# A hybrid decoder layer on one core: order of the first two weight tiles, and when the copies for the down sums are issued

## The chip, the cores and the metric

The kernel runs on one core of a Trainium2 chip. Its engines are TensorE (PE in the profile; PEld is its weight load), VectorE (DVE), ScalarE (ACT), GpSimd (POOL) and SyncE (SP), and 16 DMA engines that all queues share. The metric is the time of one execution in microseconds (us); lower is better. A kernel's time is the median of its runs.

## The reference

One decoder layer in float32 on 1024 tokens of width 1024, with 16 learned meta tokens put ahead of them:

```
h = concat([meta, x])                         # 1040 rows
proj = rmsnorm(h, norm1) @ w_in               # D_IN columns, cut into twelve parts
gdn = gated_delta(silu(conv4(gq, gk, gv)), ga, gb);  ret = retention(rotary(rq), rotary(rk), rv)
y = sigmoid(gate_a) * norm(gdn) * silu(gz) + sigmoid(gate_b) * silu(rg) * norm(ret)
h = h + y @ w_out
u = conv3(rmsnorm(h, norm2) @ w_up) + b;  a, b = split(u)
h = h + (silu(a) * b) @ w_down                # w_down is (2816, 1024)
out = rmsnorm(h, norm_f)[16:]
```

## The kernel before

**Layout.** Columns of h lie along the free axis and its channels in 8 blocks k of 128 partitions, so that a projection tile t is 128 output columns: its weights are 8 blocks of 128x128, and it needs every block of x. For accuracy each float32 operand is split into a high and a low part, and each product is three matmuls: high by high, low by high, high by low. `w_hi` is made on ScalarE (L1511), `w_lo` on VectorE (L1894), both from `w_raw`, which SP loads (512 KB, L822). Two slots hold the split weights, tile t in slot t % 2; `w_raw` has one.

**The start** (step "intro"). SP loads the 8 blocks of x. ScalarE makes `xh` of each (L1527) and its square (L1533), VectorE makes `xl` (L1916, semaphore `x_split`) and adds up the squares (L1911, `d_xss`). TensorE works on tiles 0 and 1 together while the blocks arrive; a block of a tile is 9 matmuls (`project_block`, L155), three thirds of the columns by three products. The function `first_two(s, ks)` does the blocks ks of tile s. At one place in this order stand the "ones matmuls" (L1180), which sum the squares over the channels. From their result ScalarE takes a logarithm (L1545) and an exponential (L1548); VectorE folds these roots into the rotary tables (L1942) and then does the rotary work of tiles 0 and 1 (L1946 to L1956). After it in VectorE's order stands the low split of tile 3.

**The steady state** (steps "proj", "split", "load" of a plan that all engines follow in one order). A tile is three units of 24 matmuls (L1148), one for each third of the columns. Behind each unit ScalarE copies its bank out (L1586). In the first unit of tile t ScalarE and VectorE split tile t+1, and SP issues the load of tile t+2, which waits until tile t+1 is split. Every second tile has rotary work on VectorE and two stores of 522 KB; from tile 10 on turned keys are stored too, 16 small stores for each pair of tiles (L789, L791), which SP issues ahead of the load.

**The down sums.** Late in the kernel the down projection uses sums of quarters of `w_ffn_down` (a11, a12, a21, a22, each 1408 rows of 512 columns). GpSimd prepares four of them in device memory (`down_sums`): four copies of a quarter each (L2526, 2816 KB each, device memory to device memory), issued when TensorE has finished tile 4, and from tile 65 on additions into them. `w_sums` counts all of these transfers, 16 for each; the later waits on it begin with the copies' count.

Of the kernel before, what the change touches and what calls it, by code (L numbers as in the profile page):

```python
# [17 lines left out]
KC = D // P  # L18
# [29 lines left out]
KH = FT // 2  # L48
# [59 lines left out]

BATCH = 4
NBATCH = 3  # L110
B32 = 32
INV_STEPS = 2 + 2 * (B32 - 1)

# [7 lines left out]
def shape_constants():  # L121
# [6 lines left out]
    c[:, C_EPSQ] = EPS * EPS * P  # L128
    c[:, C_BLK:C_BLK + 4] = i[:, None] // B32 == np.arange(4)[None, :]
    upto = i[:, None] <= i[None, :]  # L130
    c[:, C_TRIU:C_TRIU + P] = upto
    c[:, C_UPTO:C_UPTO + P] = np.where(upto, 0, -1e30)
    c[:, C_BELOW:C_BELOW + P] = np.where(i[None, :] < i[:, None], 0, 1e30)
    c[:, C_L5:C_L5 + 64] = -1.0 * (i[:, None] % 64 // B32 == i[None, 0:64] // B32)
    lg = np.log(1.0 - 2.0 ** (-5.0 - np.arange(RH)))
# [43 lines left out]
def front_plan():  # L179
# [52 lines left out]
    u = 34  # L232
    for b in range(NBATCH):
        steps[u].append(("tin", b))
        if b == 1:
            steps[u + 4].append(("comp", NCH - 1))
        j = 0
        while j < B32 - 1:
            u += 1
            n = min(B32 - 1 - j, 2 if u < 49 or u % 2 else 3)  # L240
            steps[u].append(("inv", b, j, j + n))
# [138 lines left out]
def third_columns(t, j):  # L380

    if t >= T_ZB or t < 8:
        return C_COL + C_N * j, C_N
    if T_Q <= t < T_V:

        return T - 344 * (3 - j), 344
    if T_K <= t:
        return (FRONT, FRONT + 348, FRONT + 694)[j], (348, 346, 346)[j]
    return N3 * j, N3
# [11 lines left out]
def program(nc, io, sc, out):  # L401

    with ExitStack() as ctx:
# [10 lines left out]
        def sem(name):  # L414
            return ctx.enter_context(nc.semaphore("f1_" + name))
# [112 lines left out]
        def w_parts(t):  # L528
# [4 lines left out]
            if 6 <= n < 8:  # L533
# [15 lines left out]
        comp, mb, xb, xc, xt = (ext[:, 5632 + 1024 * n:6656 + 1024 * n] for n in range(5))  # L549
        mbv, xbv = (x.rearrange("p (a b) -> p a b", a=B32) for x in (mb, xb))  # L550

# [11 lines left out]
               for n in range(2)]  # L563
# [7 lines left out]
        w_hi, w_lo, units_done, evac, pe_x15, d_fold = (sem(n) for n in (  # L571
            "w_hi", "w_lo", "units_done", "evac", "pe_x15", "d_fold"))
# [15 lines left out]
        d_dec, a_dec, a_eg, w_sums, pe_qk, d_attn, pe_lev, d_q5, d_x5, d_t6, a_q6, d_x6 = (  # L588
            sem(n) for n in ("d_dec", "a_dec", "a_eg", "w_sums", "pe_qk", "d_attn", "pe_lev", "d_q5", "d_x5", "d_t6",
                             "a_q6", "d_x6"))  # L590
# [40 lines left out]
        def sums_stored(j):  # L631

            return 16 * (NCH + (j + 1 if j < KH else KH + 3 * (j + 1 - KH)))
# [71 lines left out]
        def col(tab):  # L705
            return tab.rearrange("p (h o) -> p h o", o=1)
# [37 lines left out]
        def used(q):  # L744

            return (d_bank, q // KH + 1) if q % KH == KH - 1 else (d_used, (KH - 1) * (q // KH) + q % KH + 1)
# [21 lines left out]
        def tiles_done(t):  # L768
            return 3 * t + 3
# [5 lines left out]
        def _(sp):  # L775
# [22 lines left out]
            for step in plan:  # L798
                kind, a = step[0], step[1:]
# [30 lines left out]
                elif kind == "rvstore":  # L830
                    u = a[0]
                    at0, n, chunks = RV_STEPS[u - RV_A]
# [15 lines left out]
                elif kind == "kturn":  # L848
                    n = a[0] - T_K
                    store_turned(sc["kt"], n, kt, kt0, d_kt, 2 * n + 2, kt_st)  # L850
                elif kind == "vturn":
                    n = a[0] - T_V
# [70 lines left out]
                elif kind == "dl_x":  # L923
                    c = a[0]
                    if c == 0:
                        sp.wait_ge(x_st, 32 * NBATCH)
                    if c >= 2:
                        sp.wait_ge(p_exp, 2 * c - 3)
                    cols = slice(256 * (c % BATCH), 256 * (c % BATCH) + 256)
                    for odd in range(2):  # L930
                        for n in range(2):
                            to, of = 64 * odd + B32 * n, 64 * n
# [25 lines left out]
                elif kind == "dl_k":  # L958
# [3 lines left out]
                    elif c == 0:  # L962
                        sp.wait_ge(kt_st, 16 * 8 * KC)
                        sp.wait_ge(d_tout, 2 * NBATCH)
                    sp.dma_start(kd[c % 2].rearrange("p h c -> p (h c)"), sc["kt"][c]).then_inc(kd_ld, 16)
# [12 lines left out]
                elif kind == "oload":  # L978
                    n = a[0]
# [14 lines left out]
                elif kind == "gate" and a[0] < 8:  # L994
                    n = a[0]
# [49 lines left out]
            def down_operands(q):  # L1045
                p, k = q // KH, q % KH
                w = io["w_ffn_down"][0]
                first, second = w[k * P:k * P + P, :], w[(KH + k) * P:(KH + k) * P + P, :]
                into_w = (first[:, 0:512], sc["ws"][1, k], second[:, 0:512], sc["ws"][0, k], sc["ws"][2, k], sc["ws"][3, k],
                          second[:, 512:1024])[p]  # L1050
                into_a = (sc["act"][k][:, 0:512], sc["ts"][1, k], sc["act"][KH + k][:, 0:512], sc["ts"][0, k],
                          sc["ts"][2, k], sc["act"][KH + k][:, 512:1024], sc["ts"][3, k])[p]
                return into_w, into_a

            def load_down(q):
                p, k = q // KH, q % KH
                if q == KH:
                    sp.wait_ge(w_sums, 16 * (4 + 3 * KH))
                elif q == 5 * KH:
                    sp.wait_ge(w_sums, 16 * (4 + 4 * KH))  # L1060
                if q >= DIN:
                    sp.wait_ge(da_hi, q - DIN + 1)
                j = k if p == 0 else KH + k
                sp.wait_ge(act_st[j % 2], 16 * (j // 2 + 1))
                if p:
                    sp.wait_ge(sum_st, sums_stored(j))
                if q < DW:
                    sp.wait_ge(pe_p, 7 * (NPAIR - 1) if q < DEARLY else 7 * NPAIR)
                else:
                    sp.wait_ge(*used(q - DW))  # L1070
                for into, of in zip((dw_raw[q % DW], da_raw[q % DA]), down_operands(q)):
                    sp.dma_start(into[:, :], of).then_inc(dn_in[q % DIN], 16)
# [11 lines left out]
            for i in range(NPAIR):  # L1084
                j = J0 + i
# [26 lines left out]
        def _(pe):  # L1112
# [6 lines left out]
            for step in plan:  # L1119
                kind, a = step[0], step[1:]  # L1120
                if kind == "proj":
                    t, j = a
                    u = 3 * t + j
                    if T_RV <= t < T_Q:
                        pe.wait_ge(w_lo, T_RV + (4 if u < RV_B else 6 if u < RV_C else 8))
                        pe.wait_ge(evac, u - 1)
                        at0, n, chunks = RV_STEPS[u - RV_A]
# [17 lines left out]
                    at0, n = third_columns(t, j)  # L1145
# [15 lines left out]
                elif kind == "intro":  # L1161
                    pe.wait_ge(w_lo, 1)

                    def first_two(s, ks):
                        for k in ks:
                            pe.wait_ge(x_split, k + 1)
                            mm = project_block(pe, psum, 2 + 3 * s, wh[s], wl[s], xh, xl, k, 0, N3)
                            if k == KC - 1:
                                mm.then_inc(units_done, 3)

                    for k in range(KC // 2):
                        first_two(0, (k,))
                        if k == 0:
                            pe.wait_ge(w_lo, 2)
                        first_two(1, (k,))
                    first_two(0, range(KC // 2, KC))
                    pe.wait_ge(consts_in, 16)
                    pe.wait_ge(d_xss, KC - 1)
                    for bank, at0, c0, c1 in XSS:
                        mm = pe.matmul(psum[:, bank, at0:at0 + c1 - c0], ones, post[4][:, c0:c1], start=True, stop=True)  # L1180
                    mm.then_inc(pe_xss, 1)
                    first_two(1, range(KC // 2, KC))
                elif kind == "ab":
                    if a[0] == 0:
                        pe.wait_ge(evac, 3 * T_AB + 3)
# [22 lines left out]
                elif kind == "r_out":  # L1208
# [7 lines left out]
                    for h in range(RH):  # L1216
                        for e in range(2):
                            n = 2 * h + e
# [14 lines left out]
                elif kind == "r_st":  # L1233
                    c, half = a
# [225 lines left out]
            for q in range(NDOWN - TAIL):  # L1460
                p, k = q // KH, q % KH
# [426 lines left out]
        def _(dve):  # L1888
# [12 lines left out]
            for step in plan:  # L1901
# [197 lines left out]
                elif kind == "dec":  # L2099
# [4 lines left out]
                    else:  # L2104
                        dve.wait_ge(p_inv, INV_STEPS * NBATCH)
                    dve.tensor_tensor(at[c % 2], dg, col(gcum[:, c * GH:c * GH + GH]).broadcast_to((P, GH, CH)),
# [57 lines left out]
                elif kind == "tv":  # L2164
# [3 lines left out]
                    if c == 0:  # L2168
                        dve.wait_ge(d_nk, 6 * NCH + 2)
                        dve.wait_ge(p_inv, INV_STEPS * NBATCH)  # L2170
                    dve.wait_ge(v_ld, 16 * (c + 1))
# [340 lines left out]
        def _(pool):  # L2512
            pool.memset(zero, 0.0).then_inc(zero_set, 1)
            wd, rows = io["w_ffn_down"][0], KH * P
            a11, a12, a21, a22 = (wd[rows * k:rows * k + rows, 512 * m:512 * m + 512] for m in range(2) for k in range(2))
            ws = [sc["ws"][n].rearrange("k p c -> (k p) c") for n in range(4)]
# [3 lines left out]

            for step in plan:
                kind, a = step[0], step[1:]
                if kind == "proj" and a == (5, 0):
                    pool.wait_ge(units_done, tiles_done(4))
                    for into, of in zip(ws, (a21, a11, a11, a12)):
                        pool.dma_start(into, of).then_inc(w_sums, 16)  # L2526
                elif kind == "proj" and a[0] >= T_ZA and (3 * (a[0] - T_ZA) + a[1]) % 2 and 3 * (a[0] - T_ZA) + a[1] < 4 * KH:
                    k = (3 * (a[0] - T_ZA) + a[1]) // 2
                    pool.wait_ge(units_done, 3 * a[0] + a[1])
                    pool.wait_ge(w_sums, 64)  # L2530
                    n, k, of = (0, k, a22) if k < KH else (2, k - KH, a21)
                    add_block(n, k, of[k * P:k * P + P, :])
                if kind == "m_load":
# [42 lines left out]
                elif kind == "expand":  # L2576
                    c = a[0]
                    if c < 2:
                        pool.wait_ge(pe_ro, NCH)
                        pool.wait_ge(d_rS, 4 * (NCH - 1))  # L2580
                        pool.wait_ge(d_tout, 2 * NBATCH)
                    else:
# [34 lines left out]
            for j in range(FT):  # L2617
                pool.wait_ge(prod, j + 1)
                if j % KH == 0:
                    pool.wait_ge(w_sums, 16 * (4 + 2 * KH + j))  # L2620
                n, k = (1, 3)[j // KH], j % KH
                add_block(n, k, sc["ws"][n - 1 if n == 1 else 1, k])

# [84 lines left out]
```

## Time and profile before

| | us |
|---|---|
| median of 3 runs | 1974.5 |
| lowest, highest run | 1972.83, 1976.89 |
| span of the profiled execution | 1972.5 |
| TensorE busy | 1940.7 (98%) |
| VectorE busy | 1289.1 (65%) |
| ScalarE busy | 793.8 (40%) |
| GpSimd busy | 331.9 (17%) |

The page gives no time of the profiled execution other than its span, from the first to the last instruction. "Busy" is time in which at least one instruction of the engine runs. A row of the timeline gives the start, the length, the engine, the line and what is written and read; in square brackets behind it stands how long the engine was idle before it and what it waited for. Matmuls overlap in these rows: 0.32 us long, they start 0.16 us apart.

### The profile page before, as it was taken

To read this page: it belongs to the slowest core of one execution; us is meant where nothing else is said; L and a number is where in the kernel's file an instruction comes from. 1 tells how busy PE (TensorE), PEld (TensorE's weight loads), DVE (VectorE), ACT (ScalarE), POOL (GpSimd) and SP (SyncE) were. 2 spreads that over 40 slices of the span, in tenths; PEclk is the share of its full clock that TensorE was granted. 3 is DMA by queue.
4 is the path that set the end of the run, shared out by engine and by line. 5 is a ranking of instruction groups with operands and counts; after the bars stand their busy time and mean duration, and the time that the engine had idled before them with its cause. 6 is when DMAs were issued, how large, how long until landed. Compare 5 with 4: busy or idle time off the path is not lost.

```text
span 1972.5 us, 32168 instructions
## 1 busy us (share of the span) xinstructions
PE 1940.7 (98%) x13188; PEld 1874.7 (95%) x13188; DVE 1289.1 (65%) x1612; ACT 793.8 (40%) x1095; POOL 331.9 (17%) x327
## 2 busy tenths in 40 slices
PE   8999999999999989999999999999999999999998
PEld 7999998999999989999999999999999999988887
DVE  6456664747576667667633433278988889866666
ACT  5123332534333444445443333234444443445443
POOL 0000001577474122222200100200000000000001
PEclk9999999999999999999999999999999999999999
DMA  9665567654555574646436552322433545578664
GB/s 294 215 206 140 127 166 197 187 174 161 172 182 156 119 186 148 170 153 184 142 109 175 155 152 77 105 66 74 129 107 107 145 146 166 154 246 278 192 192 160
DMA packets 301223, 316.39 MB, mean 160 GB/s; under 512 B 151004, under 2 KB 220996, under 8 KB 300948
## 3 DMA queue, kind: packets, MB, share of 16 engines
q1 hardware_dynamic: 291860, 291.25, 48.2%
q0 software_dynamic: 9216, 23.07, 5.9%
q8 instruction: 105, 1.72, 0.4%
q14 instruction: 42, 0.34, 0.1%
HBM read 223.16 MB, written 114.18 MB: 171 GB/s over the span
## 4 chain that ended last, share of the span: by engine, by line
PE 89%; DVE 4%; DMA 3%; ACT 1%; issue 1%; SPq 1%; POOL 0%; DVEq 0%; POOLq 0%; ACTq 0%
PE a_psum L1148 35%; PE a_psum L1431 18%; PE a_psum L155 10%; PE a_psum L1441 10%; PE a_psum L1135 5%; PE a_psum L1223 1%; DMA w_raw<-in_w_in 1%; PE a_psum L1242 1%; PE a_psum L1328 1%; PE a_psum L1252 1%; PE a_psum L1205 1%; PE a_psum L1312 1%; PE a_psum L1220 1%; PE a_psum L1268 1%; PE a_psum L1343 1%
## 5 line engine op out<-in xcount | busy, mean ns | idle before, releaser
L1148 PE MATMUL a_psum<-xh,w_hi 128*128 128x342 f32 (+3 forms) x1656 | 537.2, 324 | 6.8 <-DVE w_lo L1894 6.8
L1148 PE MATMUL a_psum<-xl,w_hi 128*128 128x342 f32 (+3 forms) x1656 | 532.2, 321 | 0.0
L1148 PE MATMUL a_psum<-xh,w_lo 128*128 128x342 f32 (+3 forms) x1656 | 530.4, 320 | 0.0
L1148 PEld LDWEIGHTS a_psum<-xh,w_hi 128*128 128x128 f32 x1656 | 312.9, 189 | 9.3 <-DVE w_lo L1894 7.9
L1148 PEld LDWEIGHTS a_psum<-xl,w_hi 128*128 128x128 f32 x1656 | 313.1, 189 | 0.6
L1148 PEld LDWEIGHTS a_psum<-xh,w_lo 128*128 128x128 f32 x1656 | 312.9, 189 | 0.0
L1586 ACT ACTIVATE post<-a_psum 128x342 f32<-128x342 f32 (+3 forms) x207 | 94.5, 457 | 513.2 <-PE a_psum L1148 483.6
L1894 DVE TENSOR_TENSOR w_lo<-w_raw,w_hi 128x1024 fp32r<-128x1024 f32 x87 | 113.2, 1301 | 144.8 <-ACT w_hi L1511 144.8
L1511 ACT ACTIVATE w_hi<-w_raw 128x1024 fp32r<-128x1024 f32 x87 | 91.6, 1053 | 112.0 <-PE a_psum L155 64.0
L1431 PE MATMUL a_psum<-x_t_hi,up_hi 128*128 128x258 f32 x608 | 123.5, 284 | 2.7 <-DVE post L2367 2.5
L1441 PE MATMUL a_psum<-act_hi,down_hi 128*128 128x512 f32 (+1 forms) x324 | 123.6, 382 | 1.7 <-DVE act_lo L2420 1.6
L1441 PE MATMUL a_psum<-act_hi,down_lo 128*128 128x512 f32 (+1 forms) x324 | 123.5, 381 | 0.0
L1441 PE MATMUL a_psum<-act_lo,down_hi 128*128 128x512 f32 (+1 forms) x324 | 123.3, 381 | 0.0
L1431 PE MATMUL a_psum<-x_part_lo,up_hi 128*128 128x258 f32 x608 | 122.8, 283 | 0.0
L2299 DVE SCALAR_TENSOR_TENSOR post<-post,c_par,post 128x1024 f32<-128x1024 f32 x88 | 111.3, 1282 | 2.4 <-ACT post L1781 0.6
L1988 DVE SCALAR_TENSOR_TENSOR post<-post,a_par,post 128x1040 f32<-128x1040 f32 x72 | 98.7, 1371 | 2.6
L1431 PEld LDWEIGHTS a_psum<-x_t_hi,up_hi 128*128 128x128 f32 x608 | 95.0, 191 | 3.2 <-issue 2.9
L1431 PEld LDWEIGHTS a_psum<-x_part_lo,up_hi 128*128 128x128 f32 x608 | 93.9, 189 | 0.0
L2519 POOL DMA_DIRECT2D down_sums<-down_sums x22 | 17.9, 814 | 449.3 <-DVE post L2305 449.3
L1431 PE MATMUL a_psum<-x_t_lo,up_hi 128*128 128x258 f32 x456 | 92.9, 285 | 0.0
L1431 PE MATMUL a_psum<-x_b_hi,up_hi 128*128 128x258 f32 x456 | 92.0, 283 | 0.7 <-DVE u_three L2365 0.7
L1431 PE MATMUL a_psum<-x_t_hi,up_sum_lo 128*128 128x258 f32 x456 | 92.1, 283 | 0.0
(289 smaller groups left out, 3953.0 us busy)
## 6 DMA issues: line engine op xcount, KB each, us to landing
w_raw<-in_w_in SPq DMA_DIRECT2D x76, 512.0 KB, 3.9
up_raw<-in_w_up SPq DMA_DIRECT2D x19, 1024.0 KB, 4.9
mix_scratch<-post SPq DMA_DIRECT2D x32, 522.0 KB, 3.0
down_sums<-in_w_ffn_down POOLq DMA_DIRECT2D x4, 2816.0 KB, 30.4
act_scratch<-post SPq DMA_DIRECT2D x22, 512.0 KB, 2.7
down_raw<-down_sums SPq DMA_DIRECT2D x44, 256.0 KB, 2.7
act_raw<-act_sums SPq DMA_DIRECT2D x44, 256.0 KB, 3.2
ext<-mix_scratch SPq DMA_DIRECT2D x9, 1024.0 KB, 7.1
```

The costliest lines, as they stand in the source:

```text
L155: mm = pe.matmul(psum[:, bank + j, 0:n], w[:, k, :], x[:, k, col + n * j:col + n * j + n], start=(k == 0 and part == 0), stop=(k == KC - 1 ...
L1135: mm = pe.matmul(psum[0:rows_, u % 2, n * i:n * i + n], x[:, k, x0:x0 + rows_], w, start=(k == 0 and part == 0), stop=(k == KC - 1 and par ...
L1148: mm = pe.matmul(psum[:, u % 2, 0:n], w[:, k, :], x[:, k, at0:at0 + n], start=(k == 0 and part == 0), stop=(k == KC - 1 and part == 2))
L1205: mm = pe.matmul(four(7)[:, h, seen(c)], r_in[:, 8 + 2 * h + e, :], r_in[:, 2 * h + e, seen(c)], start=(e == 0), stop=(e == 1))
L1220: mm = pe.matmul(o, rvs[c % 2][:, n, :], rsc[:, h, seen(c)], start=True, stop=(c == 0))
L1431: mm = pe.matmul(region(i, n)[:, b, :], w[:, k, :], x[:, k, HP * b:HP * b + HP], start=(n < 4 and k == 0 and part == 0), stop=(k == 3 and ...
L1441: mm = pe.matmul(psum[:, (0, 4, 0, 4, 0, 4, 0)[p] + m, c0:c0 + n], a, b[:, c0:c0 + n], start=(p not in (2, 5, 6) and k == 0 and part == 0) ...
L1511: act.activation(w_parts(t)[0], wr(t), ACT.Copy).then_inc(w_hi, 1)
L1586: act.activation(dst, src, ACT.Copy).then_inc(evac, 1)
L1894: dve.tensor_tensor(lo, wr(t), hi.bitcast(F32), ALU.subtract).then_inc(w_lo, 1)
L1988: dve.scalar_tensor_tensor(out=acc[:, 0:n], in0=x, scalar=w, in1=acc[:, 0:n], op0=ALU.mult, op1=ALU.add).then_inc(d_conv, 1)
L2299: dve.scalar_tensor_tensor(out=acc_of(j, s), in0=u_out[s][:, c0:c0 + SEQ], scalar=par2[:, at0:at0 + 1], in1=acc_of(j, s), op0=ALU.mult, op ...
```

## The change

It has two parts.

The order of the start: before, blocks 0 to 3 are done in pairs (a block for tile 0, the same for tile 1), then blocks 4 to 7 of tile 0, the ones matmuls, blocks 4 to 7 of tile 1. Now blocks 0 to 5 are done in pairs, then 6 and 7 of tile 0, the ones matmuls, 6 and 7 of tile 1.

The copies: before, four at one place, behind tile 4. Now each quarter is copied in two halves of 704 rows, and one half is issued at each of the tiles 5 to 12, behind the end of the tile ahead of it. The counts that wait for the copies go from 4 to 8 transfers.

```diff
+COPIES = 8
...
             def load_down(q):
                 p, k = q // KH, q % KH
                 if q == KH:
-                    sp.wait_ge(w_sums, 16 * (4 + 3 * KH))
+                    sp.wait_ge(w_sums, 16 * (COPIES + 3 * KH))
...
-                    for k in range(KC // 2):
+                    for k in range(KC - 2):
                         first_two(0, (k,))
                         if k == 0:
                             pe.wait_ge(w_lo, 2)
                         first_two(1, (k,))
-                    first_two(0, range(KC // 2, KC))
+                    first_two(0, range(KC - 2, KC))
                     pe.wait_ge(consts_in, 16)
                     pe.wait_ge(d_xss, KC - 1)
                     for bank, at0, c0, c1 in XSS:
                         mm = pe.matmul(psum[:, bank, at0:at0 + c1 - c0], ones, post[4][:, c0:c1], start=True, stop=True)
                     mm.then_inc(pe_xss, 1)
-                    first_two(1, range(KC // 2, KC))
+                    first_two(1, range(KC - 2, KC))
...
-                if kind == "proj" and a == (5, 0):
-                    pool.wait_ge(units_done, tiles_done(4))
-                    for into, of in zip(ws, (a21, a11, a11, a12)):
-                        pool.dma_start(into, of).then_inc(w_sums, 16)
+                if kind == "proj" and 5 <= a[0] < 5 + COPIES and a[1] == 0:
+                    n, half = (a[0] - 5) // 2, (a[0] - 5) % 2 * (rows // 2)
+                    pool.wait_ge(units_done, tiles_done(a[0] - 1))
+                    pool.dma_start(ws[n][half:half + rows // 2, :], (a21, a11, a11, a12)[n][half:half + rows // 2, :]
+                                   ).then_inc(w_sums, 16)
...
-                    pool.wait_ge(w_sums, 64)
+                    pool.wait_ge(w_sums, 16 * COPIES)
```

TensorE at the start of the program, before: from the last row of tile 0's block 7 over the ones matmuls (`post_58` is the sum of the squares) into tile 1. Three rows of L155 are one block.

```order
L155 MATMUL a_psum<-xh,w_lo 128x348 x3
L1180 MATMUL a_psum<-post_58,a_cst 128x512 x2
L1180 MATMUL a_psum<-post_58,a_cst 128x20
L155 MATMUL a_psum<-xh,w_hi 128x348 x3
L155 MATMUL a_psum<-xl,w_hi 128x348 x3
L155 MATMUL a_psum<-xh,w_lo 128x348 x3
...
L1148 MATMUL a_psum<-xh,w_hi 128x342
```

Here twelve rows of L155, four blocks, stand between the ones matmuls and tile 2 (L1148); three of them are shown. In the changed kernel the same place reads:

```order
L156 MATMUL a_psum<-xh,w_lo 128x348 x3
L1181 MATMUL a_psum<-post_58,a_cst 128x512 x2
L1181 MATMUL a_psum<-post_58,a_cst 128x20
L156 MATMUL a_psum<-xh,w_hi 128x348 x3
L156 MATMUL a_psum<-xl,w_hi 128x348 x3
L156 MATMUL a_psum<-xh,w_lo 128x348 x3
L156 MATMUL a_psum<-xh,w_hi 128x348 x3
L156 MATMUL a_psum<-xl,w_hi 128x348 x3
L156 MATMUL a_psum<-xh,w_lo 128x348 x3
L1149 MATMUL a_psum<-xh,w_hi 128x342
```

The ones matmuls now stand two blocks later, with two blocks behind them, and all other matmuls of TensorE are as before.

GpSimd from its first work to the preparation of the decay matrices, before and then changed (`down_sums` is the place of the sums, the bracket names the semaphores waited for):

```order
L2513 MEMSET ext 128x1024
L2526 DMA down_sums<-in_w_ffn_down 1408x512 [waits f1_units_done]
L2526 DMA down_sums<-in_w_ffn_down 1408x512 x3
L2542 ISA
L2542 TENSOR_TENSOR post_70<-ext,gates_cum 128x1024 [waits f1_mg_ld0,f1_ab_step,f1_d_rope]
```

```order
L2514 MEMSET ext 128x1024
L2527 DMA down_sums<-in_w_ffn_down 704x512 [waits f1_units_done] x8
L2544 ISA
L2544 TENSOR_TENSOR post_70<-ext,gates_cum 128x1024 [waits f1_mg_ld0,f1_ab_step,f1_d_rope]
L2547 TENSOR_TENSOR post_70<-post_70,a_cst 128x1024 [waits f1_p_prep]
```

One wait and four copies have become eight copies of half the size, each with a wait for TensorE of its own; nothing else stands between them.

## Rows read from the trace of the kernel before

**Rows 1.** The page: the chain that ended last, and the costliest group.
```profile
PE 89%; DVE 4%; DMA 3%; ACT 1%; issue 1%; SPq 1%; POOL 0%; DVEq 0%; POOLq 0%; ACTq 0%
...
L1148 PE MATMUL a_psum<-xh,w_hi 128*128 128x342 f32 (+3 forms) x1656 | 537.2, 324 | 6.8 <-DVE w_lo L1894 6.8
```
**Rows 2.** The chain in order of time: start us, us, what.
```profile
9.22 19.71 PE a_psum L155 x108
...
90.78 12.31 DMA w_raw<-in_w_in
105.47 9.52 DMA w_raw<-in_w_in
```
**Rows 3.** Timeline of TensorE around 104 and 117 us.
```profile
104.10 0.32 PE L1148 MATMUL a_psum<-xh,w_lo 128*128 128x342 f32 x1
105.50 0.43 PE L1148 MATMUL a_psum<-xh,w_hi 128*128 128x348 f32 x1 [1.08 <-DVE w_lo L1894]
...
116.88 0.32 PE L1148 MATMUL a_psum<-xh,w_lo 128*128 128x348 f32 x1
117.38 0.43 PE L1148 MATMUL a_psum<-xh,w_hi 128*128 128x348 f32 x1 [0.18 <-DVE w_lo L1894]
```
**Rows 4.** Timeline of GpSimd and of ScalarE, 70 to 104 us.
```profile
70.84 3.60 POOL L2526 DMA_DIRECT2D down_sums<-in_w_ffn_down  x4 [69.14 <-PE a_psum L1148]
...
96.92 0.46 ACT L1586 ACTIVATE post<-a_psum 128x342 f32<-128x342 f32 x1 [3.31 <-PE a_psum L1148]
103.12 1.06 ACT L1511 ACTIVATE w_hi<-w_raw 128x1024 fp32r<-128x1024 f32 x1 [5.75 <-DMA w_raw<-in_w_in]
```
**Rows 5.** The copies' line, L2526, four transfers.
```profile
DMA to landing us min/median/max: 14.2/30.4/46.6
```
**Rows 6.** DMA queues from 80 to 120 us: packets, MB, share of the engines.
```profile
q0 software_dynamic: 2318, 9.23, 70.9%
```
**Rows 7.** The tile w_raw from 75 to 100 us, two loads.
```profile
DMA to landing us min/median/max: 11.2/11.8/12.3
```
**Rows 8.** The tile w_raw from 130 to 260 us, eleven loads.
```profile
DMA to landing us min/median/max: 3.4/3.7/4.9
```
**Rows 9.** Timeline of TensorE: block 7 of tile 0, ones matmuls, tile 3.
```profile
27.34 0.64 PE L155 MATMUL a_psum<-xh,w_hi 128*128 128x348 f32 x3
...
28.77 2.01 PE L1180 MATMUL a_psum<-post,a_cst 128*128 128x512 f32 x6
...
47.76 0.32 PE L1148 MATMUL a_psum<-xh,w_hi 128*128 128x342 f32 x1
```
**Rows 10.** Timeline of VectorE, 24 to 46 us.
```profile
24.70 1.30 DVE L1916 SCALAR_TENSOR_TENSOR xl<-y,a_par,xh 128x1044 fp32r<-128x1044 f32 x1
...
25.92 2.60 DVE L1911 TENSOR_TENSOR post<-post,post 128x1044 f32<-128x1044 f32 x2
...
33.46 2.40 DVE L1942 TENSOR_TENSOR ext<-ext 128x1044 f32<-128x1044 f32 x2 [2.12 <-ACT ext L1548]
37.81 1.25 DVE L1946 TENSOR_TENSOR post<-post,ext 128x1044 f32<-128x1044 f32 x1 [1.95 <-issue]
...
45.00 1.22 DVE L1894 TENSOR_TENSOR w_lo<-w_raw,w_hi 128x1024 fp32r<-128x1024 f32 x1
```
**Rows 11.** Timeline of ScalarE, 30 to 38 us.
```profile
30.82 1.43 ACT L1545 ACTIVATE ext<-a_psum,a_cst 128x512 f32<-128x512 f32 x3 [0.73 <-PE a_psum L1180]
32.28 1.08 ACT L1548 ACTIVATE ext<-ext 128x1044 f32<-128x1044 f32 x1
...
36.68 1.05 ACT L1540 ACTIVATE post<-a_psum 128x1044 f32<-128x1044 f32 x1 [2.39 <-PE a_psum L155]
```
**Rows 12.** Timeline of SP's issues and of TensorE, load and start of tile 13.
```profile
151.45 0.53 SPq L822 DMA_DIRECT2D w_raw<-in_w_in  x1
...
163.27 0.32 PE L1148 MATMUL a_psum<-xh,w_hi 128*128 128x348 f32 x1
```
**Rows 13.** DMA queues from 139 to 152 us: packets, MB, share of the engines.
```profile
q1 hardware_dynamic: 8372, 1.56, 65.8%
```

More of the change, by code:

```diff
@@ L1057, in load_down @@
                 if q == KH:
-                    sp.wait_ge(w_sums, 16 * (4 + 3 * KH))
+                    sp.wait_ge(w_sums, 16 * (COPIES + 3 * KH))
                 elif q == 5 * KH:
-                    sp.wait_ge(w_sums, 16 * (4 + 4 * KH))
+                    sp.wait_ge(w_sums, 16 * (COPIES + 4 * KH))
                 if q >= DIN:
@@ L2619, in _ @@
                 if j % KH == 0:
-                    pool.wait_ge(w_sums, 16 * (4 + 2 * KH + j))
+                    pool.wait_ge(w_sums, 16 * (COPIES + 2 * KH + j))
                 n, k = (1, 3)[j // KH], j % KH
```

## The prediction

> **What bounds the kernel now.** I read the page's chain and its list of costly groups first. TensorE makes up 89% of the chain that ended last, and the costliest group, the projection matmuls of L1148, sat idle for only 6.8 us in all, put down to w_lo, the low part of a weight tile [rows 1]. So only time that TensorE loses counts. The chain in order of time then says where a transfer, not TensorE, sets the pace: two loads of w_raw stand in it, 12.31 us from 90.78 and 9.52 us from 105.47 [rows 2]. TensorE's timeline shows the price: matmuls start 0.16 us apart, but between 104.10 and 105.50 lie 1.40 us, and between 116.88 and 117.38 0.50 us [rows 3]. Less the pitch that is 1.24 + 0.34 = 1.58 us lost, at the starts of tiles 8 and 9.
>
> The reason stands beside it. GpSimd issues all four copies for the down sums at 70.84 [rows 4]. They land 14.2 to 46.6 us later, the last near 120 [rows 5], and hold 70.9% of the DMA engines from 80 to 120 us, moving 9.23 MB there [rows 6]. The weight loads issued meanwhile take 11.2 and 12.3 us [rows 7]; without copies the same load takes 3.7 (3.4 to 4.9, 11 of them) [rows 8].
>
> **The copies, half by half.** The eight halves move the same 11.53 MB, 1.44 MB each. From issue to issue there is one tile of TensorE, three units of 24 matmuls at 0.157 to 0.159 us, 11.3 to 11.5 us. The first still goes out at 70.84; the others at about 82.2, 93.5, 104.3, 115.7, 127.2, 138.7 and 150.2. A half's transfer lies between two bounds: 9.23 MB in 70.9% of 40 us is 28.4 us of full engines, so 1.44 MB takes 4.4 us; and half of the first copy's 14.2 us is 7.1 us. I take 4.4, since the second has issue and two other transfers in it. Both are under 11.3, so copies no longer pile up.
>
> Load of tile 8: w_hi starts at 103.12 on the load's landing, though the unit before it had been copied out from 96.92 on [rows 4]; from there to tile 8's first matmul at 105.50 pass 2.38 us (two splits, hand-overs). Tile 8 was due at 104.26, so the load must land by 101.9; it landed at 103.1. In the changed kernel it is issued at 90.78 as before (what lets it go is the split of tile 7, which stands behind the rotary work on VectorE, not behind a transfer). The second half is gone by 82.2 + 4.4 = 86.6, by 89.3 at the high bound; the third comes at 93.5, when most of the load is through. Even if the load had to sit out a whole half, it lands at 90.78 + 3.7 + 7.1 = 101.6, in time. The stall of 1.24 us goes.
> Load of tile 9: it left at 105.47 only because tile 8's split was late. Now the split follows the copy-out at 96.92 to 97.4 and is done near 99.7, where the load leaves; at worst it lands at 110.5, with 113.4 wanted. The 0.34 us goes too. What is late next at both places is TensorE itself.
>
> Loads 10 to 12 are issued 2 us or more ahead of the next half or behind a finished one and have 6 us or more to land. The tight one is tile 13's. SP issues it at 151.45 behind 16 small stores of the turned keys [rows 12], 1.6 us earlier now (149.85), and half eight starts at 150.2. Tile 13 begins at 163.27 [rows 12], now 161.7; less 2.38, the load must land by 159.3. With 3.7 + 4.4 us it lands at 157.95, 1.3 us early; with 4.4 more for stores held up by half seven it would not (a rival, below). Cost taken: 0.
>
> GpSimd has nothing else before 150 us, so seven more waits there hold up nobody; its issues took 3.60 us for four [rows 4]. Nobody waits for the sums until the last projection tiles, some hundreds of us later: the additions wait for 128 instead of 64, long reached. So: 0.
>
> The Trainium skill, page "DMA: Bandwidth & Descriptors", section "Queues, rings and completion order", says that a DMA engine goes round robin between the queues that hold work, packet by packet. By that a load beside copies would take about twice its 3.7 us, some 7.4; rows 7 have three times that, so the trace doesn't agree with an equal share here. By the rule load 13 would land at 157.3 and cost nothing; by the 12.3 us of the row it would land at 162.2 and cost 2.9.
>
> **The pairs at the start.** TensorE's work is the same; only its order moves. A pair lets TensorE draw new blocks of x at half the speed. That pays only where it waits for x, and it doesn't: block 7's low part is ready at 24.70 + 1.30 = 26.00 [rows 10] and first used at 27.34 [rows 9], and the chain runs through TensorE's matmuls alone from 9.22 for 19.71 us, 108 of them without a transfer or another engine between [rows 2]. Gain 0.
> The three ones matmuls move back by two blocks, 2 x 1.43 = 2.87 us. Before, they came at 28.77 [rows 9], 0.25 us after the sum of squares was there (25.92 + 2.60 = 28.52 [rows 10]); now at 31.6. Behind them stands a chain: ScalarE's logarithm at 30.82 and exponential at 32.28 [rows 11], VectorE's folding of the roots into the tables at 33.46, the rotary work at 37.81 (held by ScalarE's copy of tile 1, 36.68 + 1.05), and the split of tile 3 at 45.00 + 1.22 = 46.22 [rows 10, 11]. Shifted: logarithm 33.7 to 35.1, exponential to 36.2, folding 36.3 to 38.7, rotary from 38.73, so 0.92 us later and not 2.87, since it had waited 1.95 us for tile 1. Split of tile 3 done at 47.14; tile 3 begins at 47.76 [rows 9], so 0.6 us are left. Tile 2 begins three units of 24 matmuls before tile 3, 47.76 - 11.35 = 36.4, and needs the logarithms read out of its banks, 35.1: 1.3 us left. Cost 0, with thin cover: at the full 2.87 us tile 3's split would end at 49.1 and cost 1.3.
>
> **Sum.** The page's own span is 1972.5 us; what lies around it isn't shown, and the median of the runs is 2.0 us above the span. -1.24 - 0.34 + 0 + 0 = -1.6: a span of 1970.9 and a time of 1974.5 - 1.6 = 1972.9 us. That is 0.08%. 0.2% is 3.9 us, about what a measurement of this kernel can tell from no change (the three runs lie 4.1 us apart).
>
> **Rivals.**
> (a) The load of tile 8 is as slow as before, because what slows it is its own queue, with the stores of the rotary pair just ahead of it, or any copy in flight, however short. For: three times the time and not twice [rows 7]. Against: loads of 3.7 us beside such stores later on [rows 8]. Nothing gained: 1974.5.
> (b) The stall is larger outside the profile. The 2.0 us between span and median lie in it, since transfer times vary most, and all goes: 1974.5 - 3.6 = 1970.9. Against: nothing in the profile places these 2.0 us there.
> (c) The chain behind the ones matmuls moves by its full 2.87 us: 1.6 gained, 1.3 lost, 1974.2.
> (d) The slower side: halves seven and eight fall into the time of the tiny stores. Half seven at 138.7 holds up the stores from 140 on, and SP with them, by up to 4.4 us; the load of tile 13 leaves at 154.2 and, beside half eight, takes the 12.3 us of rows 7. It lands at 166.5 where 159.3 was wanted: 7.2 us of idle TensorE, 5.6 net, 1980.1. It decides from a landing at 159.3 on, and gets slower than before from 160.9. For: SP's queue takes 65.8% of the engines from 139 to 152 us with 1.56 MB in 8372 packets, so it is the number of small pieces that fills them [rows 13]. Against: 34.2% of these 13 us is 4.4 us of full engines, just what a half needs.
> (e) The change doesn't do what it says: copies pile up again because a half takes over 11.3 us beside other work. The high bound is 7.1; then the stall stays, as in (a).
>
> **Chances.** Forecast 64%, (a) with (e) 9%, (b) 13%, (c) 7%, (d) 7%, of which 4% far enough to be slower by over 0.2%. The likeliest case alone, with the runs' scatter, is 1971 to 1975. For 8 in 10 I take 1969.5 to 1977: down past (b), up past (a) and (c) by the highest run shown. Faster by over 0.2%: most of (b)'s tail and scatter of the forecast, 0.14. Slower by over 0.2%: 0.05. Within: 0.81.
>
> **What would show it.** Right: no DMA between 82 and 125 us in the chain, tile 8 following tile 7 without a gap, loads 8 and 9 landing in under 8 us, the ones matmuls at 31.6, rotary work from 38.7, tile 3 still at 47.8, and everything from 120 us on 1.6 us earlier. Wrong: idle time of L1148 at 47.8 (c), at 104 (a), or at 161.7 with the load of tile 13 as releaser (d); or a difference that arises past 170 us, of which nothing here speaks.

## The result, and the profile after

The changed kernel is slower: median 1979.4 us (1977.3 to 1980.8) against 1974.5 us, ratio 1.0027 with a 95% interval of 1.0019 to 1.0035. The prediction was 1972.9 us, range 1969.5 to 1977.0. The profiled execution has a span of 1977.0 us, 4.5 us over that of before.

The page of the changed kernel, its chain and the group that answers to [rows 1]:

```profile
span 1977.0 us, 32172 instructions
...
PE 89%; DVE 5%; DMA 2%; SPq 2%; ACT 1%; issue 1%; POOL 0%; DVEq 0%; POOLq 0%; ACTq 0%
...
L1149 PE MATMUL a_psum<-xh,w_hi 128*128 128x342 f32 (+3 forms) x1656 | 536.8, 324 | 8.3 <-DVE w_lo L1895 8.3
```

TensorE still makes 89% of the chain, and its idle time behind w_lo has grown from 6.8 to 8.3 us. New is SPq with 2%: SyncE's issuing of transfers now sets the end for some stretch. The chain in order of time says where; it answers to [rows 2]:

```profile
36.79 90.74 PE a_psum L1149 x576
...
142.17 5.39 SPq L792
...
158.23 4.30 DMA w_raw<-in_w_in
...
164.93 24.68 PE a_psum L1149 x144
```

The two loads at 90.78 and 105.47 are gone from it: the stalls at tiles 8 and 9 don't exist any more. In their place stands one small store of turned keys, whose issue took 5.39 us, and behind it the load of tile 13. SP's timeline there, which answers to [rows 12]:

```profile
141.14 0.99 SPq L790 DMA_DIRECT2D rkt_scratch<-ext  x1
142.17 5.39 SPq L792 DMA_DIRECT2D rkt_scratch<-ext  x1
...
152.62 2.34 SPq L792 DMA_DIRECT2D rkt_scratch<-ext  x1
155.00 1.62 SPq L790 DMA_DIRECT2D rkt_scratch<-ext  x1
156.67 1.52 SPq L792 DMA_DIRECT2D rkt_scratch<-ext  x1
158.23 0.42 SPq L823 DMA_DIRECT2D w_raw<-in_w_in  x1
```

GpSimd issues half seven at 139.26 and half eight at 150.70, and SP is held just behind each. At the usual 0.5 and 0.56 us for such an issue, 4.8 us are lost behind half seven and 3.9 behind half eight (1.8, 1.1 and 1.0). The load leaves at 158.23, where 149.85 was worked out, and lands at 162.53; tile 13 wanted it by 159.3.

TensorE's timeline at tile 13:

```profile
164.93 0.66 PE L1149 MATMUL a_psum<-xh,w_hi 128*128 128x348 f32 x1 [3.08 <-DVE w_lo L1895]
165.38 0.49 PE L1149 MATMUL a_psum<-xl,w_hi 128*128 128x348 f32 x1
165.67 0.49 PE L1149 MATMUL a_psum<-xh,w_lo 128*128 128x348 f32 x1
...
168.49 0.32 PE L1149 MATMUL a_psum<-xh,w_hi 128*128 128x348 f32 x1
```

Behind the idle 3.1 us the matmuls start 0.29 us apart until 168.3, not 0.16; the granted clock from 166 to 168 us is 0.50, the 1.2 GHz level. From tile 13's first matmul to the tiles of L155/L156 (tile 15) before took 186.33 - 163.27 = 23.06 us, now 24.68: 1.62 us more.

So the account up to tile 15, which begins at 186.33 before and at 189.61 now, closes: +0.21 us at the start (tile 2's long run begins at 36.79, not 36.58; this start lies between 36.23 and 36.98 in the profiles of all runs, with the old order and the new, so the 0.21 isn't put down to the change), -1.79 for the stalls gone (1.58 by the pitch and 0.21 for the slow matmul behind each), +3.24 for the stall (164.93 where 161.69 was due), +1.62 for the clock: +3.28.

Of the 4.5 us between the two spans 1.2 remain, and the one large difference found past tile 15 is at 485. VectorE and GpSimd there, in the changed kernel and then in the kernel before (timelines):

```profile
484.49 2.54 DVE L2034 TENSOR_TENSOR y<-y 128x512 f32<-128x512 f32 x1 [8.49 <-ACT y L1647]
...
484.48 2.00 POOL L2553 TENSOR_TENSOR y<-ext,a_cst 128x1024 f32<-128x1024 f32 x1
...
490.22 1.97 PE L1243 MATMUL a_psum<-ext,y 128*128 128x256 f32 x8 [1.31 <-DVE ext L2056]
```

```profile
481.18 0.69 DVE L2033 TENSOR_TENSOR y<-y 128x512 f32<-128x512 f32 x1 [8.49 <-ACT y L1646]
...
481.45 2.28 POOL L2551 TENSOR_TENSOR y<-ext,a_cst 128x1024 f32<-128x1024 f32 x1 [0.43 <-DMA ext<-mix_scratch]
```

The same two instructions, with other neighbours in time: where GpSimd's multiply started 0.01 us ahead, VectorE's addition took 2.54 us, where it came 0.27 us behind, 0.69. TensorE then idled 1.31 us, where it idled 0.02 us in the kernel before. From tile 15 to the up projection (1194.11 before, 1198.56 now) pass 1007.8 and 1008.9 us; past that, both take 778.4.

One more idle time is larger than any named so far, and the change doesn't touch it. It stands in all thirteen profiles of this document, 4.1 to 5.0 us long, near 716 us in the kernel before, and behind it the granted clock was 0.50 from 716 to 719 us. It too waits for a load of w_raw, issued at 707.03 behind small stores and other transfers on SP and landed 6.46 us later:

```profile
715.89 0.66 PE L1148 MATMUL a_psum<-xh,w_hi 128*128 128x342 f32 x1 [5.01 <-DVE w_lo L1894]
```

### The profile page after: what moved, and what is told of

Its sections match the earlier page's. It is cut to its first block, busy times and chain, and to the rows that moved or that the text cites. A ratio compares the mean times of both kernels' runs of the same rounds, so it can differ in the third digit from the quotient of the medians.

```text
span 1977.0 us, 32172 instructions
## 1 busy us (share of the span) xinstructions
PE 1940.6 (98%) x13188; PEld 1874.0 (95%) x13188; DVE 1296.6 (66%) x1612; ACT 794.8 (40%) x1095; POOL 335.1 (17%) x331
## 4 chain that ended last, share of the span: by engine, by line
PE 89%; DVE 5%; DMA 2%; SPq 2%; ACT 1%; issue 1%; POOL 0%; DVEq 0%; POOLq 0%; ACTq 0%
PE a_psum L1149 35%; PE a_psum L1432 18%; PE a_psum L156 10%; PE a_psum L1442 10%; PE a_psum L1136 5%; PE a_psum L1224 1%; PE a_psum L1243 1%; PE a_psum L1329 1%; PE a_psum L1253 1%; PE a_psum L1206 1%; PE a_psum L1313 1%; PE a_psum L1221 1%; SPq L792 1%; PE a_psum L1269 1%; PE a_psum L1344 1%
```

## The experiments

Two theories stood at first. **Held stores**: halves seven and eight hold up the small stores of turned keys on SP's queue, and with them the load of tile 13. **Start order**: the later ones matmuls cost. Smaller questions were the clock and the two instructions at 485. All comparisons are with runs of the kernel before on the same chip.

| run | median, us | kernel before, us | ratio, 95% interval | tile 15 begins, us | idle before tile 13, us |
|---|---|---|---|---|---|
| changed kernel | 1979.4 | 1974.5 | 1.0027 (1.0019 to 1.0035) | 189.61 | 3.1 |
| e1 pairs only | 1974.2 | 1974.1 | 1.0005 (0.9996 to 1.0015) | 186.21 | 0 |
| e2 copies only | 1980.3 | 1974.1 | 1.0031 (1.0020 to 1.0041) | 190.71 | 3.6 |
| e3 copies early | 1973.0 | 1974.1 | 0.9997 (0.9989 to 1.0006) | 184.95 | 0 |
| e4 changed kernel again | 1980.5 | 1974.1 | 1.0038 (1.0025 to 1.0051) | 191.32 | 4.8 |
| e5 half seven moved | 1974.0 | 1974.1 | 0.9999 (0.9990 to 1.0009) | 185.87 | 0.9 |
| e6 half eight moved | 1974.2 | 1974.1 | 1.0005 (0.9995 to 1.0014) | 185.01 | 0.2 |
| e7 stores behind the load | 1972.9 | 1974.1 | 0.9996 (0.9987 to 1.0006) | 184.81 | 0 |
| e8 filler matmuls | 1978.1 | 1974.1 | 1.0023 (1.0013 to 1.0032) | 189.54 | 1.1 |
| e9 early, port in order | 1973.8 | 1974.9 | 0.9991 (0.9981 to 1.0000) | 184.46 | 0 |
| e10 before, port in order | 1974.4 | 1974.9 | 0.9993 (0.9984 to 1.0002) | 185.70 | 0 |
| e11 before, other order | 1975.3 | 1974.9 | 1.0003 (0.9995 to 1.0012) | 185.01 | 0 |

**e1, the start order alone.** Edit, on the kernel before:

```diff
-                    for k in range(KC // 2):
+                    for k in range(KC - 2):
...
-                    first_two(0, range(KC // 2, KC))
+                    first_two(0, range(KC - 2, KC))
...
-                    first_two(1, range(KC // 2, KC))
+                    first_two(1, range(KC - 2, KC))
```

Expected: 

> The order of the first two tiles alone, with the four copies as before. My theory (the loss comes from the copies) expects no change beyond 0.3 us: the ones matmuls at 31.6 to 31.8 us instead of 28.8, the split of tile 3 done near 47.3, tile 3 still beginning near 47.8, and both stalls at the starts of tiles 8 and 9 still there; 1974.7 us. The rival that the start order costs expects most of the 4.9 us here, about 1979.

Measured: ratio 1.0005, no difference that can be told, no idle TensorE between 40 and 60 us, and the stalls at tiles 8 and 9 still there (1.4 us together). The start order is cleared. Its one profiled execution is long (1977.6 us, above the median), with the late addition at 485 in it.

**e2, the copies alone.** Edit: the rest of the diff, with the halves at tiles 5 to 12.

Expected: 

> The eight half copies at tiles 5 to 12 alone, with the start as before. Theory: the whole loss is here. No stall at tiles 8 and 9 (1.6 us gained), SP held for 4 to 6 us at a small store of turned keys just behind half seven and for some 3 us more behind half eight, the load of tile 13 issued 8 us later than without them, TensorE idle for about 3 us before tile 13 and then for some 3.5 us at half its clock (1.7 us more): about +3.3 us at 200 us, and 1978.5 to 1979.5 in all if GpSimd's rotary multiply again starts just ahead of VectorE's addition near 484 us (1.3 us more), 1977.7 if not. Rival (the start order costs): 1973 to 1975.

Measured: ratio 1.0031; the whole loss is here. SP was held 5.15 us at its fourth small store and again behind half eight, the load left at 158.31, TensorE idled 3.6 us. The addition at 485 took 0.69 us this time, and yet the median is 1980.3, over the 1977.7 expected then: the stall and its low clock came to more than I had taken from one profile (tile 15 at +4.4 us against before, not +3.3). The other 1.5 us of the median's excess are not accounted for.

**e3, the same halves earlier.** Edit on e2, counting three units to a tile:

```diff
+            HALF_AT = {15: [0], 17: [1], 19: [2], 21: [3], 23: [4], 25: [5], 27: [6], 29: [7]}
...
-                if kind == "proj" and a == (5, 0):
-                    pool.wait_ge(units_done, tiles_done(4))
-                    for into, of in zip(ws, (a21, a11, a11, a12)):
-                        pool.dma_start(into, of).then_inc(w_sums, 16)
+                if kind == "proj" and 3 * a[0] + a[1] in HALF_AT:
+                    pool.wait_ge(units_done, 3 * a[0] + a[1])
+                    for g in HALF_AT[3 * a[0] + a[1]]:
...
```

Expected: 

> The same eight halves, but one behind every second unit from tile 5 on (every 7.6 us), so that the last is issued near 125 us and landed by 134, before the first store of turned keys at 140; the start as before. Theory (the collision of halves seven and eight with the small stores makes the loss): no stall at tile 13, and the stalls at tiles 8 and 9 mostly gone as well: 1.6 us faster than before, 1972.9; if halves 7.6 us apart still delay the load of tile 8 past 101.9 us, 1974.5. Rival (copies in halves are dearer as such, or any spreading costs): slower than before by 2 us or more.

Measured: 1973.0 us, tile 15 at 184.95, 1.38 us ahead of before; no stall at tiles 8, 9 or 13. The ratio doesn't tell it from before. Halving the copies is not dear; their place is. The queues show how. First the changed kernel from 140.2 to 147 us, then e3 from 140.5 to 147 (packets, MB, share of the engines; q0 carries GpSimd's copies, q1 SP's transfers):

```profile
q0 software_dynamic: 361, 1.43, 67.5%
q1 hardware_dynamic: 1750, 0.25, 21.8%
```

```profile
q1 hardware_dynamic: 5303, 0.66, 66.7%
```

The stores move 1750 packets beside a half and 5303 without one. A packet of the copy has 4 KB, one of these stores some 0.13 KB. Worked out from the shares, a packet of the copy holds an engine for some 0.20 us, and one of the stores for 0.013 to 0.014 us with or without the copy beside it. So a store's packet isn't slower beside the copy; the stores get 21.8% of the engines' time instead of 66.7%. How the engines pick between the two queues no run shows.

**e4, the changed kernel again.**

Expected: 

> The changed kernel again, on the same chip as the other three. Both theories: 4 to 5 us slower than before, about 1979. Its profile tells whether the stall at tile 13 (3 us, half clock behind it) and the late addition near 484 us (1.3 us) come back: theory expects the first every time; the second hangs on two instructions that started 0.01 us apart and may be missing, which would make the span 1.3 us shorter.

Measured: ratio 1.0038. The stall came back, larger (4.8 us idle, SP held 6.03 us), tile 15 at +5.0 us. The late addition did not: 0.69 us. So the late addition belongs to that one profile, not to the change; and e2, where it is early, takes 1008.7 us from tile 15 to the up projection, nearly the 1008.9 of the changed kernel, so that the 1.2 us are its doing is not shown. The stall and the clock are 3.3, 4.4 and 5.0 us at tile 15 in the three profiles (changed kernel, e2, e4), against 4.9, 6.2 and 6.4 us between the medians. Where the rest comes from is not shown; past tile 15 two profiles with the copies of the kernel before, its own and e1's, differ by 5 us.

**e5 and e6, one half moved.** The tables in place of e2's:

```diff
-            HALF_AT = {15: [0], 18: [1], 21: [2], 24: [3], 27: [4], 30: [5], 33: [6], 36: [7]}
+            HALF_AT = {15: [0], 18: [1], 21: [2], 24: [3], 27: [4], 30: [5, 6], 36: [7]}     # e5
+            HALF_AT = {15: [0], 18: [1], 21: [2], 24: [3], 27: [4], 30: [5, 7], 33: [6]}     # e6
```

Expected of e5: 

> Half copies alone as in e2, but half seven goes out together with half six at tile 10 (about 127.5 us), so that none is in flight when the small stores of turned keys begin at 140; half eight stays at tile 12. Theory (half seven holds SP at its small stores for 5 to 6 us and that makes the load of tile 13 late): no such hold at 142, the stores are issued by about 150, the load of tile 13 leaves near 150 and shares with half eight, landing by 158; no stall at tile 13, 1.6 us under before. Rival (half eight beside the load is what matters): the stall stays at 2 to 3 us or more, 1977 to 1979.

Expected of e6: 

> Half copies alone as in e2, but half eight goes out with half six at tile 10; half seven stays at tile 11. Theory (both halves hold SP, seven by 5 us and eight by 3 us): SP loses 5 us at 142, the stores end near 155, the load of tile 13 lands near 159, just at its limit of 159.3: a stall of 0 to 1 us, 1973 to 1974.5. Rival (half seven alone makes the whole stall): as in e2, 1978 or more. Rival (half eight alone): no stall and no long hold.

SP's timeline, e5:

```profile
141.91 1.87 SPq L792 DMA_DIRECT2D rkt_scratch<-ext  x1
...
144.89 1.95 SPq L790 DMA_DIRECT2D rkt_scratch<-ext  x1
...
152.20 0.42 SPq L823 DMA_DIRECT2D w_raw<-in_w_in  x1
```

and e6:

```profile
142.62 4.75 SPq L792 DMA_DIRECT2D rkt_scratch<-ext  x1
...
154.65 0.53 SPq L823 DMA_DIRECT2D w_raw<-in_w_in  x1
```

In e5 the long hold is gone. Two short ones remain: the first ends when the load of tile 12, slow at 7.4 us from 136.4 on beside the doubled halves, lands at 143.8; for the second, from 144.89, the trace shows no reason. The load of tile 13 leaves at 152.2, meets half eight and takes 8.1 us, landing at 160.3: 0.9 us idle. In e6 SP is held 4.75 us, the load leaves at 154.65, takes under 5 us and leaves 0.2 us idle. So it takes both halves: with either one alone at its place the load leaves by 154.7 and at most 0.9 us are lost; with both it leaves at 158.2 to 159.1 (changed kernel, e2, e4, e8). e5 was expected to have no stall; 0.9 is a miss.

**e7, the stores behind the load.** Edit on the changed kernel, on SP alone:

```diff
-                elif kind == "rturn":
+                elif kind == "rturn" and a[0] != 4:
...
                     sp.dma_start(wr(t), weights_of(t)).then_inc(w_seen(t)[0], 16)
+                    if t == 13:
+                        for n in range(0, 2):
+                            store_turned(sc["rkt"], n, rt[n % 2], rt0[n % 2], d_rt, 2 * n + 2, rt_st)
```

Expected: 

> The changed kernel with one edit on SP: the 16 small stores of the first pair of turned keys stand behind the load of tile 13, not ahead of it. All eight halves stay at their tiles. Theory (the load is late because it stands behind stores that are held): the load of tile 13 leaves near 145.6 and lands by 150 to 153, no stall at tile 13 and none at half clock; 1972.9 plus whatever the later stores cost, at most 1974.5. Rival (the halves slow the load itself or VectorE): the stall at tile 13 stays, 1978 or more.

Measured: 1972.9 us. SP's timeline:

```profile
145.58 0.33 SPq L823 DMA_DIRECT2D w_raw<-in_w_in  x1
...
152.43 2.18 SPq L792 DMA_DIRECT2D rkt_scratch<-ext  x1
...
155.20 3.77 SPq L792 DMA_DIRECT2D rkt_scratch<-ext  x1
```

The halves stay where the change has them, the stores are still held, now by half eight (issues of 2.18 and 3.77 us), and nothing is lost: the load lands in 4.2 us, tile 13 starts on time, tile 15 at 184.81. The load now also leaves before half eight is issued, at 150.77, so e7 alone doesn't part the two; but in the changed kernel the load itself took only 4.30 us. Together they settle the way of the loss: not the engines' bandwidth for the load, but its place in SP's order behind stores that a copy starves.

**e8, TensorE kept busy in the stall.** Edit on the changed kernel:

```diff
+                    if u == 39:
+                        for n in range(24):
+                            pe.matmul(psum[:, 6, 0:348], wh[0][:, n % KC, :], xh[:, n % KC, 0:348], start=True, stop=True)
                     if j == 0:
                         pe.wait_ge(w_lo, t + 1)
```

Expected: 

> The changed kernel with 24 matmuls of 348 columns added ahead of TensorE's wait for tile 13; they compute something nobody reads, into a bank that nobody uses then, and take 3.8 us. Theory (TensorE falls to half its clock because it stood idle, which costs 1.7 us or more behind the stall of 3 to 5 us): the fillers lie inside the stall, the matmuls of tile 13 run 0.16 us apart from the first on, and the kernel is about 1 to 2 us faster than the changed kernel, 1977 to 1978.5. Rival (the low clock comes from elsewhere, such as the transfers, or the filler itself is in the way): tile 13 still starts at 0.29 us a matmul and the time is equal or up to 1 us worse than 1979.4.

Windows of e8 and then of the changed kernel (PE, PEld, DVE, ACT, POOL busy, PEclk, DMA share, GB/s):

```profile
164.00:166.00 2.00, 1.33 (x9) 1.04 (x7) 0.90 (x1) 1.76 (x3) 0.00 (x0) 1.00 0.84 342
166.00:168.00 2.00, 1.61 (x10) 1.62 (x11) 2.00 (x4) 0.00 (x0) 0.00 (x0) 1.00 0.33 68
```

```profile
164.00:166.00 2.00, 1.07 (x4) 1.07 (x5) 2.00 (x3) 0.31 (x1) 0.00 (x0) 0.74 0.41 87
166.00:168.00 2.00, 2.00 (x9) 2.00 (x9) 1.34 (x4) 0.00 (x0) 0.00 (x0) 0.50 0.73 243
```

With the fillers the granted clock stays at 1.00 and tile 13 to tile 15 takes 189.54 - 166.38 = 23.16 us, without them 24.68 (e4: 25.23, e2: 25.55). So the low clock behind the stall costs 1.5 to 2.4 us, and it follows from the idle time. The median, 1978.1, is 1.2 and 2.4 us below the two measurements of the changed kernel, but each was measured beside its own runs of the kernel before and the intervals of the ratios overlap: the trace shows the gain, the medians don't prove it.

**e9, e10 and e11, the two instructions at 485.** In the ten profiles up to here, VectorE's addition took 2.4 to 2.5 us in the four where GpSimd's multiply had started first (changed kernel, e1, e6, e7) and 0.69 us in the six others. e9 is e3, and e10 the kernel before, with GpSimd made to come second; e11 is the kernel before with VectorE made to come second:

```diff
                     pool.wait_ge(pe_ro, c)
+                    if c == 2:
+                        pool.wait_ge(d_ros, 2 * c - 1)     # e9, e10
...
                     dve.wait_ge(a_ros, ros(c, 1))
+                    if c == 1:
+                        dve.wait_ge(p_rqd, c + 2)          # e11
```

Expected of e9: 

> The early halves of e3 with one wait more on GpSimd: the rotary multiply of the third chunk waits until VectorE's addition near 484 us is done, so that GpSimd can't start first. Theory (in the profiles so far VectorE's addition took 2.4 instead of 0.7 us exactly where GpSimd's multiply had started first, and TensorE then idled 1.2 us): addition 0.7 us every time, no idle of TensorE at L1243 near 485 but a remnant of 0.6; as fast as the best profile of e3, 1.6 us or a little more below before: 1971.5 to 1973. Rival (GpSimd, busy for 28 of 30 us there, becomes late itself by the wait): 1974 or more.

Expected of e10: 

> The kernel before with that wait alone. Theory: it can gain only in those runs in which GpSimd would have started first (4 of 10 profiles of all kernels so far), 1.3 us each: 0.5 us on the median, 1973.6. Rival (GpSimd becomes late): 1975 or more.

Expected of e11: 

> The kernel before with the opposite order forced: VectorE's addition of the second chunk waits for the end of GpSimd's multiply. Theory (what costs is that VectorE's chain starts 2 us late): TensorE idles 1.2 to 1.9 us near 487, span 1.3 to 2 us over that of e10, about 1975.3. Rival (the late addition is hidden in most runs): equal to e10 within 0.5 us.

In e9 and e10 the addition takes 0.69 us and TensorE idles 0.3 us there; in e11 it starts at 482.21 behind the multiply, and TensorE idles 2.0 us. The spans differ less, 1971.8 and 1972.7 in e10 and e11, medians 1974.4 and 1975.3: 0.9 us, where 1.3 to 2 were expected. Part of the delay is caught up before the up projection. The ratios' intervals overlap, and tile 15 begins 0.7 us earlier in e11 than in e10, so the worth of the order in the median is not shown. e9 has the lowest ratio of all runs, 0.9991 with an interval that ends at 1.0000: some 1.8 us or 0.1% under before, at the edge of what can be told.

## Why the prediction was wrong, point by point

- **What bounds the kernel, and the stalls at tiles 8 and 9: right.** They vanished, as did the long loads (3.5 to 4.6 us now). Their worth of 1.6 us was read from one profile, and is not the same in each. From tile 2's long run to tile 15 pass 147.96 to 147.97 us in e3, e7 and e9, which have no stall, and 149.75, 149.86, 149.11 and 148.46 in the four profiles with the copies of the kernel before (before, e1, e10, e11). So 0.5 to 1.9 us were to be had, 1.3 in the mean; as times, e3 and e7 can't be told from the kernel before.
- **The pairs at the start: right.** The ones matmuls came at 31.83 (31.6 forecast), rotary work at 38.96 (38.73), split of tile 3 done at 47.38 (47.14), no idle time; e1 shows no effect.
- **The copies' length: too short.** A half carries 1.43 MB in 4.6 us of full engines (67.5% of 6.8 us), close to the 4.4 taken. But from issue to landing it is in flight 6.8 to 9.0 us, 8.1 in the median, over the high bound of 7.1. Under 11.3 it stays, so the copies don't pile up.
- **"Cost taken: 0" for the load of tile 13: this step failed.** The sum let the load leave at 149.85, as if no half held up the stores ahead of it on SP; it left at 158.23. The one reason given, against rival (d), was an average: the stores leave 34.2% of 13 us free, 4.4 us, "just what a half needs". The average doesn't say who gets the engines while both want them: beside half seven the stores had 21.8% of them, where alone they take 66.7%. Rival (d) had the mechanism, and 7%. Of its terms the hold behind half seven was 4.8 us (4.4 given); missing was the second hold, 3.9 us, since stores that seven had held were still there when eight came; the load then took 4.3 us, not 12.3, as it left when eight was through; and missing was the clock, 1.6 us here. The stall was 3.2 us against 7.2, the net +3.3 to tile 15 against +5.6. That (d)'s time of 1980.1 is within 1 us of the measured 1979.4 and 1980.5 is luck: too long a load made up for the terms that it lacked.
- **The rule weighed against the trace.** The Trainium skill, "DMA: Bandwidth & Descriptors", section "Queues, rings and completion order", says that an engine takes turns between queues packet by packet. I applied it to the load only, where a share by turns among packets of like size would give twice the time and the rows gave three times. It bears on the stores: if the packets that the profile counts took turns one for one, the stores would move as many as the copy, 361, and by 0.13 KB against 4 KB a thirtieth of its bytes. The trace doesn't show that: they moved 1750, 4.8 for each of the copy's and a sixth of its bytes. The same section takes a packet as several descriptors, drained together, and no run shows whether the profile's packets are those; so the rule is neither borne out nor refuted here.
- **Chances.** Slower by over 0.2% had 0.05. What spoke for (d), the packet count of [rows 13], was in the text, and the margin worked out for the load was 1.3 us with one known term, the stores, left out of it. With hindsight, a thin margin on the path with an unpriced term should have had more, by my judgment some 0.3.

What is open: why the stall differs from one execution to the next (3.1, 3.6, 4.8 us), and where inside the stretch from tile 15 to the up projection the other microsecond or two of run-to-run difference come from. From the up projection on the traces point at one source: near 1303 us TensorE idles 1.4 to 2.2 us in every profile. In e1 and e4, the two in which it idled longest (1.9 and 2.2), the granted clock of the next 3 us was 0.75 and 0.51, and from the up projection to the end they took 2.0 and 2.2 us longer than in the kernel before.

## What to carry to other kernels

Spreading a bulk copy thin removes a pile-up, but check each new place of a piece against what the other queues do there, and not by bytes or a mean share over a long stretch: here small-piece stores got a third of their usual share of the engines beside large packets. A load that the critical engine waits for should not stand behind such stores in its queue's order; e7 took the whole loss away by moving the stores behind the load. And where two engines start on each other within a few hundredths of a microsecond, one profile can show a difference that no change has made.

## What the runs showed of the hardware

- Stores in pieces of 128 bytes moved 1750 packets in 6.8 us beside a copy with packets of 4 KB from device memory to device memory, and 5303 in 6.5 us without it: a third. The time from issue to landing of those of L790 was 5.7 us in the median and up to 7.3 beside the copy, 2.5 and up to 3.2 without one.
- SP got only about three of these stores ahead when a half was in flight at their start: in e2, e4, e6, e8 and the changed kernel alike the long issue is the fourth (4.75 to 6.03 us), and everything in SP's order behind it waits.
- TensorE idle for 3.1 to 4.8 us came back at the 1.2 GHz level for 3.4 us or more, 1.5 to 2.4 us dearer; idle for 1.1 us (before, tile 8; e8) or 0.9 us (e5) it came back at full clock. Between them it went either way: behind the same idle time of 2.5 us near 1375 to 1383 us the granted clock of the next 3 us was 0.50 to 0.51 in seven profiles, 0.70 in one and 1.00 in five.
- A GpSimd multiply of 128x1024 that reads local memory and starts first made a VectorE addition of two local operands wait: 2.4 to 2.5 us in place of 0.69, ending 0.55 us behind the end of the multiply, which took 2.0 us (484.48 + 2.00 + 0.55 = 487.03). Started second but within the addition, the multiply took 2.1 to 2.4 us.
